# High half of the gated tiles after the weights' split, two tiles kept in SBUF, mixer loads later

## What is computed

```python
proj = jnp.einsum('btd,de->bte', h, w_in[l])
q, k, v, r, a_lr, su, sv, g_a, g_b = jnp.split(proj, IN_SPLITS, axis=-1)
z = jnp.einsum('btr,rk->btk', a_lr, w_alpha_up[l]) + b_alpha[l]
...
def block(args):                       # PEER, after the top-16 choice
    xx, ii, gg = args
    u = expert_down[ii]
    a = jax.nn.gelu(jnp.einsum('pd,ped->pe', xx, u), approximate=False)
    vv = expert_up[ii]
    return jnp.einsum('pe,ped->pd', gg * a, vv)
...
def _swiglu(h, w_gate, w_up, w_down):
    return (jax.nn.silu(h @ w_gate) * (h @ w_up)) @ w_down
```

## Time and profile before

| | us |
|---|---|
| median of 3 runs (2665.69 to 2669.61) | 2666.11 |
| the profiled execution, its own time | 2664.01 |
| its span in the trace | 2662.3 |
| PE busy | 2271.7 |
| DVE busy | 1734.9 |
| ACT busy | 1157.7 |

### The profile page before, as it was taken

The page is one execution under the profiler, slowest core; times in us unless marked ns, Lnnn a source line. Parts: engine busy times, 40 slices in busy tenths (PEclk is TensorE's granted clock), DMA queues, the critical chain, the costliest instruction groups (busy, mean ns, idle before and its releaser), DMA issues.

```text
span 2662.3 us, 37886 instructions
## 1 busy us (share of the span) xinstructions
PE 2271.7 (85%) x14738; PEld 2029.0 (76%) x14738; DVE 1734.9 (65%) x3401; ACT 1157.7 (43%) x1906; POOL 53.9 (2%) x65
## 2 busy tenths in 40 slices
PE   2888889999978888888897789799879996697997
PEld 2777889999956666778785557698878886566997
DVE  5576579899956666766665657566666654664554
ACT  2433444555533434444344345544444444454444
POOL 0000000000000000000000000000000000000000
PEclk8898999999989999989996879899989997888999
DMA  7565546654456666756561110367656663102563
GB/s 251 186 210 179 179 142 203 202 183 149 149 188 219 219 217 211 244 177 203 172 200 46 48 48 17 111 218 228 207 171 203 215 208 121 64 1 72 175 186 122
DMA packets 138546, 435.55 MB, mean 164 GB/s; under 512 B 15424, under 2 KB 38720, under 8 KB 137856
## 3 DMA queue, kind: packets, MB, share of 16 engines
q1 hardware_dynamic: 109424, 396.93, 46.4%
q10 hardware_dynamic: 26352, 24.49, 2.7%
q0 software_dynamic: 2592, 11.70, 1.2%
HBM read 419.17 MB, written 13.89 MB: 163 GB/s over the span
## 4 chain that ended last, share of the span: by engine, by line
PE 54%; DVE 21%; issue 11%; ACT 10%; DMA 2%; POOL 1%; ACTq 0%; POOLq 0%; SPq 0%; DVEq 0%
PE bk L1610 51%; DVE SPL L1037 7%; ACT SPL L702 5%; DVE R L1037 2%; PE bk L1616 2%; DVE RAW L1071 2%; DVE TMP L1037 2%; ACT WHL L702 2%; DMA RAW<-in_ada 1%; ACT R L702 1%; DVE WHL L1037 1%; ACT R L704 1%; DVE EXT L1071 1%; DVE R L1046 1%; DVE ST L1052 1%
## 5 line engine op out<-in xcount | busy, mean ns | idle before, releaser
L1037 DVE TENSOR_TENSOR SPL<-RAW,SPL 128x1024 fp32r<-128x1024 f32 (+1 forms) x614 | 742.1, 1218 | 543.4 <-ACT SPL L702 541.2
L1610 PE MATMUL bk<-HH,SPL 128*128 128x256 f32 x3840 | 762.8, 292 | 65.2 <-DVE SPL L1037 52.2
L702 ACT ACTIVATE SPL<-RAW 128x1024 fp32r<-128x1024 f32 (+1 forms) x614 | 632.6, 1047 | 280.4 <-PE bk L1610 211.4
L1610 PEld LDWEIGHTS bk<-HH,SPL 128*128 128x128 f32 x3840 | 631.4, 197 | 80.6 <-issue 59.0
L1610 PE MATMUL bk<-SPL,WHL 128*128 128x512 f32 x2328 | 581.2, 405 | 71.2 <-DVE SPL L1037 56.9
L1610 PEld LDWEIGHTS bk<-SPL,WHL 128*128 128x128 f32 x2328 | 446.7, 196 | 174.4 <-issue 77.1
L1610 PE MATMUL bk<-HL,SPL 128*128 128x256 f32 x1920 | 552.6, 288 | 0.0
L1610 PEld LDWEIGHTS bk<-HL,SPL 128*128 128x128 f32 x1920 | 378.6, 197 | 1.7 <-issue 0.2
L1610 PE MATMUL bk<-SPL,HH 128*128 128x256 f32 (+1 forms) x1664 | 331.1, 301 | 48.6 <-DVE SPL L1037 36.2
L702 ACT ACTIVATE R<-bk 128x512 f32<-128x512 f32 (+5 forms) x376 | 186.7, 508 | 393.0 <-PE bk L1610 343.9
L1610 PEld LDWEIGHTS bk<-SPL,HH 128*128 128x128 f32 x1664 | 282.5, 209 | 56.4 <-issue 41.2
(11 more groups left out here) (117 smaller groups left out, 2027.5 us busy)
## 6 DMA issues: line engine op xcount, KB each, us to landing
RAW<-in_peer SPq DMA_DIRECT2D x256, 512.0 KB, 4.6
RAW<-in_ada SPq DMA_DIRECT2D x144, 512.0 KB, 4.5
RAW<-in_ffn SPq DMA_DIRECT2D x132, 512.0 KB, 4.4
RAW<-in_win SPq DMA_DIRECT2D x96, 512.0 KB, 4.6
RAW<-in_ffd SPq DMA_DIRECT2D x66, 512.0 KB, 4.1
RAW<-in_wout SPq DMA_DIRECT2D x32, 512.0 KB, 4.5
kept<-TMP ACTq DMA_DIRECT2D x90, 128.0 KB, 3.3
TMP<-kept ACTq DMA_DIRECT2D x90, 128.0 KB, 4.7
```

The source lines that it names most:

```text
L702: ins = e.activation(out, in_, func, bias=bias, scale=scale)
L1037: e.tensor_tensor(out, a, b, op).then_inc(*dve.up(*points))
L1610: ins = e.matmul(out, lhsT, rhs, start=start, stop=stop, skip_group_check=True)
```

## The change

1. **Kept tiles.** The multiplication by the gates is made one tile ahead (`pm` of the next tile), and the high half is taken in a step `ph` of its own, which stands behind `pu` and so behind the split of the weights.
2. **Late tiles.** `ph` of tile k - 1 stands between `pd` of tile k and `pu` of tile k - 2; the multiplication of tile k stands behind that `pu`.
3. **SwiGLU.** The same with a step `fz`: the halves of tile j - 1 are taken between the two products of tile j. The products' bank alternates between 4 and 5; bank 5 is taken out of the rotations of the steps that run beside it.
4. **Order of the tiles.** Tiles 88 and 89, whose gelu comes last, are used first and straight from `early`; they are neither stored nor loaded.
5. **`sil2(0)`.** Its load is issued in the third kept step and the silu (now `sil3`) in the seventh, in place of both ahead of the first tile.
6. **The start.** `walr` and `wau` are loaded first of all; the mixer's other loads (three rows spread over 128 partitions, and `sgw`) wait for `A1`. `alr` is a split product too: 24 matmuls of fp32r in place of 8 of fp32, with one copy on ACT and one subtraction on DVE for its halves.

```diff
@@ ffn_steps
-        out += [("fh", l, s, j, n) for n in range(2)] * (j < NF) + [("fs", l, s, j)] * (j < NF)
-        out += [("fy", l, s, j - LAG)] * (j >= LAG)
+        out += [("fh", l, s, j, 0)] * (j < NF) + [("fz", l, s, j - 1)] * (1 <= j <= NF)
+        out += [("fh", l, s, j, 1), ("fs", l, s, j)] * (j < NF) + [("fy", l, s, j - LAG)] * (j >= LAG)
@@ make_plan
-    plan += [("pl", j) for j in range(2)] + [("sil2", 0)]
-    peer = []
-    for j in range(P + LAG):
-        peer += [("pl", j + 2)] * (j + 2 < NA) + [("pm", j)] * (j < NA) + [("pd", j)] * (NA <= j < P)
-        peer += [("pu", j - LAG)] * (j >= LAG) + take(j >= 6 and (j % 4 == 0 or (j > NA and j % 2 == 1)))
+    peer = [("pm", SEQ[0])]
...
+    for k in range(P + LAG):
+        kept = k < NA
+        peer += tile("pl", k + 2, k + 2 < NA) + tile("pd", k, NA <= k < P)
+        peer += tile("pm", k + 1, k + 1 < NA) + tile("ph", k - 1, NA < k <= P)
+        peer += tile("pu", k - LAG, k >= LAG)
+        peer += tile("ph", k, kept) + tile("pm", k, NA <= k < P)
+        peer += [("sil2", 0)] * (k == 2) + [("sil3", 0)] * (k == 6)
+        peer += take(k >= 7 and (k % 4 == 0 or (k > NA and k % 2 == 1)))
...
+SEQ = [NA - 2, NA - 1] + list(range(NA - 2)) + list(range(NA, P))
@@ hid_act
+            if key in (("peer", NA - 2), ("peer", NA - 1)):
+                return early(key[1])
@@ POOL: sil, sil2, mix_in
+                load("walr", walr, dram["walr"][:, :])
+                load("wau", wau[0:16, :], dram["wau"][:, :])
                 pool.wait_ge(T.at("cons"))
...
-                    pool.wait_ge(T.at("full", ("g", 63)), T.at("kept", NA - 1), T.at("kept", NA - 2))
+                    pool.wait_ge(T.at("full", ("g", 63)), T.at("kept", NA - 3), T.at("hl", ("peer", NA - 2)),
+                                 T.at("hl", ("peer", NA - 1)))
...
-                load("walr", walr, dram["walr"][:, :])
-                load("wau", wau[0:16, :], dram["wau"][:, :])
+                pool.wait_ge(T.at("A1"))
@@ ACT: pe, pd, fs
+                if j >= NA - 2:
+                    return
...
                 A(hid_act(key), ps("pd", j)[:, 0:256], ACT.Gelu, ("out", ("pd", j)), ("gelu", j))
-                hidden_hi(key)
...
                 A(hid_act(key), ps("fs", l, s, j)[:, 0:256], ACT.Silu, ("silu",) + key)
-                hidden_hi(key)
@@ PE: rotations, alr, fh
-            PROJ = {(0, 1): (6, 7), (0, 0): (5, 6, 7), (1, 0): (5, 6, 7), (1, 1): (5, 6, 7)}
+            PROJ = {(0, 1): (6, 7), (0, 0): (5, 6, 7), (1, 0): (5, 6, 7), (1, 1): (6, 7)}
...
-            REST = {(0, 1): (0, 1, 2), (0, 0): (5, 6, 7), (1, 0): (5, 6, 7)}
+            REST = {(0, 1): (0, 1, 2), (0, 0): (6, 7), (1, 0): (5, 6, 7)}
...
-                    mm(b[0:16, 0:256], v2(walr, 8)[:, k, :], v2(ht, 8)[:, k, :], k == 0, k == 7,
-                       *((("full", ("alr",)),) if k == 7 else ()))
+                    for q, (x, y) in enumerate(pairs([w[:, 16 * k:16 * k + 16] for w in walr2], [h[:, k, :] for h in H[0]])):
...
-                b = take(key, (4,)) if n == 0 else ps(*key)
+                b = take(key, (4, 5)) if n == 0 else ps(*key)
```

More of the change, by code:

```diff
@@ L100 @@
     "pick": "topk", "selT": "topk",
-    "oh": "gate", "g": "gate", "pe": "early", "pl": "peer", "pm": "peer", "pd": "peer", "pu": "peer", "peer_out": "peer",
+    "oh": "gate", "g": "gate", "pe": "early", "pl": "peer", "pm": "peer", "ph": "peer", "pd": "peer", "pu": "peer", "peer_out": "peer",
 }
@@ L226, in make_plan @@
     late = ada_steps(l0, range(16)) + [("mods", 0, "a")] + ada_steps(l0, range(16, 48))
-    last = [("sil2", 1)] + ada_steps(l1, range(48))
+    last = [("sil2", 1), ("sil3", 1)] + ada_steps(l1, range(48))
     plan = [("sil",)] + ada_steps(first, range(6)) + [("norm_a", "h1")] + ada_steps(first, range(6, 12))
@@ L282, in make_plan, with tile @@
             n += 1
-    plan += [("pl", j) for j in range(2)] + [("sil2", 0)]
-    peer = []
-    for j in range(P + LAG):
-        peer += [("pl", j + 2)] * (j + 2 < NA) + [("pm", j)] * (j < NA) + [("pd", j)] * (NA <= j < P)
-        peer += [("pu", j - LAG)] * (j >= LAG) + take(j >= 6 and (j % 4 == 0 or (j > NA and j % 2 == 1)))
+    peer = [("pm", SEQ[0])]
+    def tile(kind, k, given):
+        return [(kind, SEQ[k])] if given else []
+    for k in range(P + LAG):
[6 more added lines that the diff above has]
+        peer += take(k >= 7 and (k % 4 == 0 or (k > NA and k % 2 == 1)))
     cut = peer.index(("pd", 102))
@@ L294, in make_plan @@
     plan += weave(chain + qkv_steps(0, 0, True), attend_steps(0, 1)) + attend_steps(0, 0)
-    side = weave(out_steps(0, 1) + pre_steps(0, 1) + ffn_steps(0, 1), last[:25])
+    side = weave(out_steps(0, 1) + pre_steps(0, 1) + ffn_steps(0, 1), last[:26])
     plan += weave(out_steps(0, 0) + pre_steps(0, 0), side) + [("mods", 1, "a")]
     kv1 = [("norm_k", (1, 1, "a")), ("norm_b", (1, 1, "a"))] + qkv_steps(1, 1, False)
-    ffn = weave(ffn_steps(0, 0), last[25:])
+    ffn = weave(ffn_steps(0, 0), last[26:])
     plan += ffn[:24] + weave(ffn[24:], kv1) + [("mods", 1, "f")]
@@ L563, in program @@
         for step in PLAN:
-            if step[0] in ("pm", "pd", "fs"):
+            if step[0] in ("pm", "fs"):
                 hidden[step[1:] if step[0] == "fs" else ("peer",) + step[1:]] = len(hidden)
@@ L733, in sil_, with sil3 @@
                 A(crow, crow, ACT.Silu, ("crow",))
-            def sil2(l):
+            def sil3(l):
                 act.wait_ge(T.at(f"crow2_{l}"))
@@ L757, in nT, with mix_in @@
                     A(Hs[0][:, :, c], ht3[:, :, c], ACT.Copy, ("hH", t, i))
+            def mix_in():
+                act.wait_ge(T.at("walr"))
+                A(walr2[0], walr, ACT.Copy, ("walr_hi",))
             def qk(j):
@@ L875, in pe_ @@
                     act.wait_ge(T.at("kept", j - 2))
-                A(a, ps("pe", j)[:, 0:256], ACT.Gelu, ("out", ("pe", j)))
+                A(a, ps("pe", j)[:, 0:256], ACT.Gelu, ("out", ("pe", j)), ("gelu", j))
+                if j >= NA - 2:
+                    return
                 act.wait_ge(act.own)
@@ L1012, in fo @@
                     A(v2(QS[(l, s)]["oY"], 2)[:, i, 512:1024], ps(*key), ACT.Copy, ("out", key))
-            steps = {"sil": sil_, "sil2": sil2, "norm_a": norm_a, "nT": nT, "qk": qk, "decay": decay,
+            steps = {"sil": sil_, "sil3": sil3, "norm_a": norm_a, "nT": nT, "mix_in": mix_in, "qk": qk, "decay": decay,
                      "v": project("v", vt, ACT.Copy), "sv": project("sv", sv, ACT.Gelu), "su": project("su", su, ACT.Gelu),
@@ L1186, in nT, with mix_in @@
                 tt(Hs[1][:, :, c], ht3[:, :, c], Hs[0][:, :, c].bitcast(F32), ALU.subtract, ("hT", t, i))
+            def mix_in():
+                dve.wait_ge(T.at("walr_hi"))
+                tt(walr2[1], walr, walr2[0].bitcast(F32), ALU.subtract, ("walr_lo",))
             def alr():
@@ L1671, in alr @@
                 b = take(("alr",), MIX)
-                pe.wait_ge(T.at("walr"), T.at("hT", "h1", 1))
+                pe.wait_ge(T.at("walr_lo"), T.at("hT", "h1", 1))
                 for k in range(8):
-                    mm(b[0:16, 0:256], v2(walr, 8)[:, k, :], v2(ht, 8)[:, k, :], k == 0, k == 7,
-                       *((("full", ("alr",)),) if k == 7 else ()))
+                    for q, (x, y) in enumerate(pairs([w[:, 16 * k:16 * k + 16] for w in walr2], [h[:, k, :] for h in H[0]])):
+                        last = k == 7 and q == 2
+                        mm(b[0:16, 0:256], x, y, k == 0 and q == 0, last, *((("full", ("alr",)),) if last else ()))
             def qk(j):
@@ L1807, in pu @@
             def pu(j):
-                if j == 0:
+                if j == SEQ[0]:
                     for c in range(4):
                         take(("py", c), (c,))
-                second_product(("peer", j), CHUNKS[("pu", j)][0], [ps("py", c) for c in range(4)], j == 0, j == P - 1,
+                second_product(("peer", j), CHUNKS[("pu", j)][0], [ps("py", c) for c in range(4)], j == SEQ[0], j == P - 1,
                                *((("full", ("py",)),) if j == P - 1 else ()))
```

31 lines of the change are left out of this document (13 added, 18 removed).

## The result

The changed kernel takes **2622.5 us** (median of 4, 2621.2 to 2630.8); the kernel before, timed beside it, 2667.9 (4 runs). The ratio is 0.9836, with a 95% interval of 0.9812 to 0.9859. The forecast was 2632, with a range of 2600 to 2654. The profiled execution took 2622.2 us, its span is 2620.5.

A forecast was written before the change was run, and what follows sets the result against it. PE, busy 85% of the span, was taken as the bound, its roughly 390 us idle winnable. Terms -5 - 10 + 0 - 8 - 5.6 - 7 + 1.5 = -34 us gave 2630 on the profiled execution, 2632 as median; range 2600 to 2654.

The forecast's parts named there:

- Start: Start of the kernel: moving 2 MB of mixer loads behind `A1` saves 5 us; the `alr` split counts 0.
- Between the stages: Before the kept tiles: PE's 13.58 us standstill shrinks, since tile 88 is in SBUF; -10 us, from -12 to -6.
- Kept tiles: Kept tiles: shorter serial loop offset by loads having one step to land; four steps 14.5 us against 14.45, so 0.
- the loop of 12.3: Kept tiles: serial loop through DVE and ACT, about 12.3 us for four steps if loads are never late; -42 us.
- L: Kept tiles: time a tile's load takes, set at 4.7 us; four steps take 2L + 5.1.
- L + 2.0: Kept tiles: loop through the load for two steps; L + 3.1 where two modulation products replace the split.
- rival A: Kept tiles: loads are quick; at 3.7 us four steps take 12.5, -38 more, 2594 us; chance 0.20.
- Late tiles: Late tiles: weights come 0.55 us earlier, PE's gap falls from 0.94 to 0.39 at 14 places; -8 us, 0 to -13.
- SwiGLUs: SwiGLUs: six bank waits go, -5.6 us; eight weights' waits nearly go, -7; smaller bank rotations cost +1.5.
- B: Kept tiles: loads a little slower, 5.1 us each, +17 us, 2649 us; chance 0.13.
- C: Kept tiles: loads above 5.7 us eat all gains, slower than before; at 6.0, +53 us, 2685 us; chance 0.07.
- D: Late tiles and SwiGLUs keep their gaps because the next chunk isn't there; 2647 us; chance 0.08.

The follow-up runs named there:

- e5: Changed kernel with the mixer's loads no longer waiting for the last product of `A1`: 2629.5 us, ratio 0.9860 to the kernel before.
- e1: Changed kernel with the kept tile's product back in its own step, high half still behind the weights' split: 2575.9 us, ratio 0.9669 to the kernel before.
- e4: Changed kernel with the SwiGLU's products in bank 4 alone and the old rotations of three banks: 2635.9 us, ratio 0.9895 to the kernel before.
- e10: Changed kernel with the second network's silu put back right behind its load: 2609.9 us, ratio 0.9791 to the kernel before.
- e2: Changed kernel with the late tiles in the old order (gelu, product, high half of the same tile, weights' split): 2646.0 us, ratio 0.9938 to the kernel before.
- e6: Changed kernel with tiles in natural order, 88 and 89 stored and loaded again, silu steps left as changed: 2620.6 us, ratio 0.9830 to the kernel before.
- e7: Changed kernel with the new steps (`fz`, `sil3`) weighing 0 instead of 0.3 in the planner: 2614.6 us, ratio 0.9810 to the kernel before.

## Why the prediction was right, and where it was not

**Start, -5:** right, -5.4, and e5 gives 5.1 back. The forecast had `A1` near 38.5; it is at 37.94.

**Between the stages, -10:** right, -9.7. The first kept product is at 723.41, earlier than the 726 of the forecast, and 1.9 us of that is the early products' gain, which had no term.

**Kept tiles, 0:** the size is right (four steps 14.4 us, forecast 14.5), and so is the mechanism in the main: the loads take the place of the loop that was cut (DVE waits for them; e1 shows the loop of 12.3 behind it). The formula isn't right. I took one mean L, 4.7, for all loads and two of them in four steps. What happens is that most loads (62%) take at most 4.2 us, and for those the loop through the load (L + 2.0, so 5.8 for two steps at the median) is no longer than the serial one (2 x 3.1 = 6.2), so they cost nothing. One in four, issued ahead of the two modulation products, takes 5 to 5.8 and stands on the chain. Four steps are L of that one load plus 9.3. By the prediction's own formula the median of 3.8 would have given 2 x 3.8 + 5.1 = 12.7 us, near rival A's 12.5 and its 38 us, and the mean of the 74 loads, 4.3, would have given 13.7; the loads were that quick, and the gain didn't come. So the criterion that the text gave for being wrong ("the loads' median leaves 4.3 to 5.1") was met while the term was right: the forecast had a slower load in a formula that counts every load, the kernel has quick ones and one slow one that counts. That both come to 14.4 is partly luck. The slow load is the one behind three crowded chunks.

The sentences on the Trainium skill, "DMA: Bandwidth & Descriptors", come out so: the estimate of 2.3 us from "Anatomy of one DMA" is below every load of the stage (3.6 at least), and the 42 us of gain that it would have given were not there. That section gives its figures for transfers that POOL issues, and these loads are issued by ACT, so the estimate was of another path. The order of completions that the same page states agrees with the trace: none of the 74 loads lands before the chunk issued ahead of it. No run isolated it.

**Late tiles, -8:** too small; -16.3 us. The mechanism is the forecast's: the gap went from 0.94 to 0.34 (forecast 0.39). The count failed. I counted 14 plain gaps of 0.94 us until 1279 us; the trace has 12. The woven tiles that follow have them until 1390 us, and at two of the woven tiles the gap was 2.30 us and is now 0.78. In the list of PE's gaps over 0.25 us from 1052 to 1457 us (before) and the same stretch of after, the sum falls from 62 to 51 us, 11 of the 16; the other 5 are not traced to a wait.

**SwiGLUs, -12.6 with banks and order, less 1.5 for rotations:** too small; -23.3, or some 21 without the moved work. In the woven two, ten waits of DVE's low half went where I counted eight, and all five for the bank where I counted four; one of 2.8 us for `HCL` became one of 1.9. PE's gaps add to 60.3 us before (1738 to 2265) and 46.0 after, 14.3 of the 19.7. The other 5.5 us are PE's busy time, 466.7 against 461.2 us at the same mean clock (0.94). Of these 1.9 are the 15 matmuls that start ahead of the stretch in the changed kernel. Some 2.6 more are an estimate: a matmul's row lasts 0.28 us while the next one starts 0.11 us after it, so each of the 16 waits over 0.25 us that are gone (26 before, 10 after) had about 0.16 us in the busy time too. The rest, about 1 us, stays open. What the smaller rotations cost was not separated: e4 undoes them together with the second bank, and its 11 us are the two taken together.

**The step that failed outright** is one that the prediction didn't have: the change part by part listed the steps that were moved and didn't ask what `weave` makes of a list with more entries. Between 1480 and 1738 us the changed kernel lost 14.7 us: 8 for the second silu, which got a place of its own in the list, some 4 to 5 for the weights of the new steps, and the 1.9 of moved work. The three errors (-8, -12, +15) nearly cancel, which is why 2632 was close to 2622.5. The forecast's size is right partly by luck, and so is the exact zero in the kept tiles; the signs of the start, the gap between the stages, the late tiles and the SwiGLUs are not.

**The rivals.** A: its condition (quick loads) came for most of them, its gain not. B and C: L did not rise. D: the gaps went, though the transfers had to come faster.

## What to carry to other kernels

When a step is made earlier in a software pipeline, ask of every buffer that it reads how many steps its load then has: here one line that moved a product of 0.4 us up by a tile cost 45 us, more than the whole change gave. Where a planner places steps by weights, splitting a step in two can move everything that is woven with it: give the new part no weight, and look at what the old step stood next to. And when parts that are undone one by one cost more than the whole gave, look for a loss in the change as well as for an overlap: here, of the 27 us between 68 and 41, the loss is about 13, the overlap of order and banks about 6, and the remaining 8 are not traced. When two traces are compared stage by stage, count the instructions of each stage too, or moved work passes for a loss or a gain.

## What the runs showed of the hardware

The loads of 128 KB mostly take one of two times in the changed kernel, 3.6 to 4.0 or 4.7 to 5.8 us. In e1, where four of them are issued in 12.3 us instead of 14.4, the median moves from 3.8 to 5.0. In both, a load lands just behind the 512 KB chunk issued ahead of it (in the median 0.33 us behind it, in e1 0.19), and the chunks ahead of the loads take 3.8 us in the median, in e1 5.2.

One stretch runs at two speeds from execution to execution. Two windows of the changed kernel (columns: window, length, PE busy with its matmuls, granted clock, share of the DMA engines, GB/s):

```profile
2010.00:2020.00 10.00, 8.09 (x46) 0.70 0.65 222
2020.00:2030.00 10.00, 10.00 (x59) 0.79 0.52 153
```

The same stretch in e10, 7 us earlier:

```profile
2003.00:2013.00 10.00, 8.07 (x64) 1.00 0.66 207
2013.00:2023.00 10.00, 10.00 (x71) 1.00 0.79 256
```

PE has the same two short waits there (1.3 and 1.9 us) in both, 70 us behind a standstill of 11.6. In one execution part of the next 20 us is granted the lower of the two clock levels (1.2 GHz instead of 2.4), in the other not, and the difference is about 5 us. e2, e6, e7 and e10 have it at full clock, the kernel before and the other runs have not, and e6 differs from the changed kernel only hundreds of us earlier. What decides it no run shows. So a comparison of two executions can be off by 5 us in this way, more than several of the parts studied here are worth; the issue times by place tell the two apart.
